# All products of a decoder block with the pass of the low weights last

## The chip, the cores and the metric

The kernel runs on one core of a Trainium2 chip. The metric is the device time of one execution in microseconds, the median of several runs. The core has a matrix engine (TensorE, PE in the profile; its weight loads are PEld), VectorE (DVE), ScalarE (ACT), GpSimd (POOL), and SyncE (SP), which here issues all large transfers. The engines run their own instruction streams in order and meet at semaphores.

## The reference

One decoder block over 1024 tokens with a model width of 1024, in float32. A combined projection gives q, k, v, the conv inputs and the gates. A gated short convolution and a sliding-window attention are merged by sigmoid gates and share the output projection. A SwiGLU FFN of width 2816 follows. Both sub-layers end with a scaled residual and a layer norm.

```python
proj = jnp.einsum('bsd,de->bse', x, w_in[l])
q, k, v, cb, cc, ch, g_conv, g_attn = jnp.split(proj, SPLIT_POINTS, axis=-1)
y_conv = short_conv_mixer(cb, cc, ch, conv_w[l])
y_attn = sliding_window_attention(q, k, v, attn_sinks[l])
merged = jax.nn.sigmoid(g_conv) * y_conv + jax.nn.sigmoid(g_attn) * y_attn
mix = jnp.einsum('bse,ed->bsd', merged, w_out[l])
x = layer_norm(ALPHA * x + mix, ln1_g[l], ln1_b[l])
hid = jax.nn.silu(jnp.einsum('bsd,df->bsf', x, w_gate[l])) * jnp.einsum('bsd,df->bsf', x, w_up[l])
ffn = jnp.einsum('bsf,fd->bsd', hid, w_down[l])
x = layer_norm(ALPHA * x + ffn, ln2_g[l], ln2_b[l])
```

## The kernel before

Every large product is made in three passes over float32r operands. A matrix w is held as w_hi, its rounded value, and w_lo = w - w_hi; the activations likewise as a_hi and a_lo. A product adds w_hi·a_hi, w_hi·a_lo and w_lo·a_hi in one PSUM bank of 128 x 512. `product` (line 1435) does this for one tile of 128 output channels and one half (512) of the tokens: for each of 8 depth tiles (2 for the down projection) three matmuls, lines 1441, 1442, 1443. A product of the projections is thus 24 matmuls. `project` calls it for the input projection, `project_out` for the output projection, `gate_up` and `down` for the FFN. `pair_product` has its own loop of 4 depth tiles with the lines 1662, 1663, 1664; it is one of seven such products by which a pair of halves of gate and up is built, in a loop that takes four of them a pass. `low_last` (line 1425), used for half 0 of the output projection alone, already has another order: lines 1428 and 1429 over all depth tiles, then a wait, then line 1432 eight times.

The high part of a weight tile is copied by ScalarE (semaphores w_hi_s, fw_hi_s, wd_hi_s, ph_s, lines 661, 791, 763, 847, 882) and the low part subtracted by GpSimd after it (w_lo_s, fw_lo_s, wd_lo_s, pl_s, lines 511, 555, 531, 586, 602). `product` is entered after a wait for the low part, which includes the high one. The raw tile is loaded anew when its low part is done.

The order of the work is written out by hand for each engine. Some products have a hook that is called before each depth tile t. In the first product it places transposes of x (`turn_x`), and it waits for parts of the activations: x_lo_s in the first product, m_lo_s in all of half 1 of the output projection (v = 8 to 15), n_lo_s in the first gate/up product of each half. The same hook puts the small matmuls of the first layer norm into the stream (`weave`): the mean over channels (line 1562) before tile 2 of product v=9, the sum of squares (line 1570) before tile 7 of v=11, the spread of the inverse deviation (line 1578) before tile 4 of v=12; and for half 1 of the tokens the same at tile 5 of the first gate/up product and at tiles 3 and 6 of the third:

```python
for v in range(DT, 2 * DT):
    project_out(1, v, v, out_bank(v), {DT + 1: {2: lambda: mean(0)}, DT + 3: {7: lambda: variance(0)},
                                  DT + 4: {4: lambda: spread(0)}}.get(v, {}))
head_hooks = {0: {5: lambda: mean(1)}, 2: {3: lambda: variance(1), 6: lambda: spread(1)}}
```

What these wait for is made elsewhere. VectorE makes the low part of the merged activations, m_lo (line 985), adds a finished output product to the residual (`out_sum`, line 1188), centres (line 1152), adds odd squares (line 1147), scales (line 1176) and makes the low part act_lo (line 1164). ScalarE squares and copies high parts (line 785). GpSimd sums channels (`channel_sum`, line 544) and adds even squares (line 551). Around the first down products VectorE also makes sums and differences of activations for the pair products (line 1259, whose low parts are GpSimd's line 632) and adds the down products to the residual (`add_down`, line 1267); a down product v waits, from v = 4, for sum v-4 to have freed its bank.

Of the kernel before, what the change touches and what calls it, by code (L numbers as in the profile page):

```python
# [106 lines left out]
def build(nc, x, w_in, conv_w, sinks, w_out, ln1_g, ln1_b, w_gate, w_up, w_down, ln2_g, ln2_b, out):  # L107
    ctx = ExitStack()
    with ctx:  # L109
# [185 lines left out]
        def unit_bank(u):  # L295
            return u % 3
# [1126 lines left out]
        def _(pe):  # L1423
# [11 lines left out]
            def product(bank, w_h, w_l, a_hi, a_lo, tiles, ready=None):  # L1435

                for t in range(tiles):
                    if ready is not None:
                        ready(t)
                    hi, lo = folded(a_hi(t)), folded(a_lo(t))  # L1440
                    pe.matmul(bank, w_h(t), hi, start=(t == 0), stop=False)  # L1441
                    pe.matmul(bank, w_h(t), lo, start=False, stop=False)  # L1442
                    last = pe.matmul(bank, w_l(t), hi, start=False, stop=(t == tiles - 1))  # L1443
                return last

            def project(slot, h, bank, ready=None):
                return product(ps[:, bank, :], lambda t: w_hi[:, slot, t], lambda t: w_lo[:, slot, t],
                               lambda t: act_hi[:, t, half(h)], lambda t: act_lo[:, t, half(h)], DT, ready)
# [45 lines left out]
            for n, (t, h) in enumerate(PRO_UNITS):  # L1494
                pe.wait_ge(w_lo_s, t + 1)
# [10 lines left out]
                project(t % 2, h, unit_bank(n + 1), hook).then_inc(unit_s, 1)  # L1506
# [4 lines left out]
            with pe.Fori(0, NKV) as k:  # L1511
                for step, n in STEPS:
                    if step == "unit":
                        if n % 2 == 0:
                            pe.wait_ge(w_lo_s, k * NT + (PRO_TILES + n // 2 + 1))
# [6 lines left out]
                        project((n // 2) % 2, n % 2, unit_bank(n)).then_inc(unit_s, 1)  # L1522
# [59 lines left out]
            def project_out(h, v, w, bank, at={}):  # L1582

                pe.wait_ge(res_s, v + 1)
                if h == 0:
# [5 lines left out]
                pe.wait_ge(w_lo_s, v + (IN_TILES + 1))  # L1591
                return product(ps[:, bank, :], lambda t: out_hi(w)[:, t], lambda t: out_lo(w)[:, t],
                               lambda t: m_hi[h][:, t], lambda t: m_lo[h][:, t], DT,
                               weave(at, lambda t: pe.wait_ge(m_lo_s, DT * h + t + 1))).then_inc(out_s, 1)
# [8 lines left out]
            def gate_up(h, s, ready=None):  # L1603

                if h == 0:
                    pe.wait_ge(fw_lo_s, s + 1)
# [3 lines left out]
                        ready).then_inc(f_s, 1)  # L1610

            def down(i, c, h, m):

                v = h * DT + m
                if m == 0:
                    pe.wait_ge(wd_lo_s, i * 4 + (2 * c + 2))
# [4 lines left out]
                if v >= 4:  # L1621
                    pe.wait_ge(add_s, i * 32 + (16 * c + v - 3))
                product(ps[:, 4 + v % 4, :], lambda t: wd_hi[:, t, blk(m)], lambda t: wd_lo[:, t, blk(m)],
                        lambda t: hid_hi[:, t, half(h)], lambda t: hid_lo[:, t, half(h)], 2).then_inc(d_s, 1)
# [15 lines left out]
            def pair_product(i, c, j):  # L1640
# [4 lines left out]
                pe.wait_ge(pl_s, i * 28 + (n + 1))  # L1645
# [13 lines left out]
                for t in range(4):  # L1659
                    hi, lo = ring(w_hi, n)[:, t], ring(w_lo, n)[:, t]  # L1660
                    b_hi, b_lo = (folded(ap) for ap in right(j, t))
# [70 lines left out]
```

## Time and profile before

| | |
|---|---|
| median of 3 runs | 1383.12 us (1382.83 to 1383.79) |
| the profiled execution, its own time | 1382.94 us |
| its span, first to last instruction | 1381.1 us |
| TensorE busy | 1367.6 us, 6658 matmuls |
| VectorE / GpSimd / ScalarE busy | 780.9 / 596.4 / 484.2 us |
| mean granted TensorE clock | 0.999 |
| moved by DMA | 80.22 MB |

The times of the profile are microseconds from the start of the span; a line number is that of the kernel's text. "idle before" is the time in which the engine did nothing just before an instruction, with what released it. Matmuls are pipelined, and the end of one overlaps the next, so their pace is read from start to start.

### The profile page before, as it was taken

What the parts mean: (1) busy time and instruction counts of PE and PEld (TensorE: products, weight loads), DVE (VectorE), ACT (ScalarE), POOL (GpSimd) and SP (SyncE); (2) the same over time, 40 slices, a digit from 0 to 9 for tenths busy, and PEclk for the clock granted to TensorE, in tenths of its full rate; (3) what the DMA queues carried; (4) which work ended last, traced back from release to release, by engine and by line L of the source; (5) the groups of instructions that cost most, each with busy time, mean ns of one, the idle gap of its engine ahead of it and who ended that gap; (6) DMA issues with size and microseconds to landing.
All of it is one profiled execution on the core that took longest, in us unless ns stands there. A gap on an engine that the chain in (4) does not pass through costs nothing. (4 is left out here: it accounts for less than half of the span.)

```text
span 1381.1 us, 19035 instructions
## 1 busy us (share of the span) xinstructions
PE 1367.6 (99%) x6658; PEld 1201.5 (87%) x6658; DVE 780.9 (57%) x1196; ACT 484.2 (35%) x932; POOL 596.4 (43%) x375
## 2 busy tenths in 40 slices
PE   9999999999999999999999999999999999999997
PEld 8888888888888888888888888888888888888886
DVE  3137564566447653767967935645456454464547
ACT  4434333343243433345245332322323213233143
POOL 2222223212322132124884483754737547475474
PEclk9999999999999999999999999999999999999999
DMA  6111111111111111111430121112211122121113
GB/s 184 57 51 47 34 43 47 44 46 46 46 46 33 43 46 46 46 46 51 132 93 31 46 80 43 61 47 67 68 31 61 53 61 68 32 66 56 52 54 122
DMA packets 128406, 80.22 MB, mean 58 GB/s; under 512 B 8432, under 2 KB 123120, under 8 KB 128368
## 3 DMA queue, kind: packets, MB, share of 16 engines
q1 hardware_dynamic: 128368, 79.73, 19.0%
q8 instruction: 22, 0.36, 0.1%
q14 instruction: 16, 0.13, 0.0%
HBM read 75.53 MB, written 4.19 MB: 58 GB/s over the span
## 5 line engine op out<-in xcount | busy, mean ns | idle before, releaser
L511 POOL TENSOR_TENSOR w_lo<-raw,w_hi 128x1024 fp32r<-128x1024 f32 x54 | 128.3, 2377 | 481.4 <-ACT w_hi L661 481.4
L1441 PE MATMUL ps<-act_hi,w_hi 128*128 128x512 f32 x864 | 329.5, 381 | 1.1 <-DVE act_lo L971 1.1
L1442 PE MATMUL ps<-act_lo,w_hi 128*128 128x512 f32 x864 | 327.7, 379 | 0.0
L1443 PE MATMUL ps<-act_hi,w_lo 128*128 128x512 f32 x864 | 327.7, 379 | 0.0
L602 POOL TENSOR_TENSOR w_lo<-raw,w_hi 128x512 fp32r<-128x512 f32 x80 | 110.3, 1378 | 204.7 <-ACT w_hi L882 204.7
L1443 PEld LDWEIGHTS ps<-act_hi,w_lo 128*128 128x128 f32 x864 | 163.4, 189 | 23.1
L1441 PEld LDWEIGHTS ps<-act_hi,w_hi 128*128 128x128 f32 x864 | 163.4, 189 | 23.0 <-issue 1.3
L1442 PEld LDWEIGHTS ps<-act_lo,w_hi 128*128 128x128 f32 x864 | 163.6, 189 | 21.6
L1441 PE MATMUL ps<-hid_hi,wd_hi 128*128 128x512 f32 x320 | 121.6, 380 | 1.3 <-DVE res L1267 1.3
L1442 PE MATMUL ps<-hid_lo,wd_hi 128*128 128x512 f32 x320 | 121.4, 379 | 0.0
L1663 PE MATMUL ps<-act_lo,w_hi 128*128 128x512 f32 x320 | 121.4, 379 | 0.0
L1664 PE MATMUL ps<-act_hi,w_lo 128*128 128x512 f32 x320 | 121.4, 379 | 0.0
L1443 PE MATMUL ps<-hid_hi,wd_lo 128*128 128x512 f32 x320 | 121.4, 379 | 0.0
L1662 PE MATMUL ps<-act_hi,w_hi 128*128 128x512 f32 x320 | 121.3, 379 | 0.0
L1273 DVE TENSOR_TENSOR res<-res,ps 128x512 f32<-128x512 f32 x128 | 87.3, 687 | 59.9 <-PE ps L1443 59.9
L1663 PE MATMUL ps<-a_lo,w_hi 128*128 128x512 f32 x240 | 91.0, 379 | 0.0
L1664 PE MATMUL ps<-a_hi,w_lo 128*128 128x512 f32 x240 | 91.0, 379 | 0.0
L1662 PE MATMUL ps<-a_hi,w_hi 128*128 128x512 f32 x240 | 91.0, 379 | 0.0
L602 POOL TENSOR_TENSOR w_lo<-w_sum,w_hi 128x512 fp32r<-128x512 f32 x60 | 80.7, 1353 | 9.2 <-ACT w_hi L882 9.2
L661 ACT ACTIVATE w_hi<-raw 128x1024 fp32r<-128x1024 f32 x54 | 57.0, 1055 | 62.6 <-PE ps L1443 62.1
L1118 DVE TENSOR_TENSOR pt_lo<-ps,pt_hi 128x512 fp32r<-128x512 f32 x60 | 38.9, 687 | 64.0 <-ACT pt_hi L741 63.0
L882 ACT ACTIVATE w_hi<-raw 128x512 fp32r<-128x512 f32 x80 | 49.8, 623 | 71.2 <-POOL raw L614 50.6
(205 smaller groups left out, 2514.7 us busy)
## 6 DMA issues: line engine op xcount, KB each, us to landing
raw<-in_w_in SPq DMA_DIRECT2D x52, 512.0 KB, 3.6
raw<-in_w_gate SPq DMA_DIRECT2D x40, 256.0 KB, 2.8
raw<-in_w_up SPq DMA_DIRECT2D x40, 256.0 KB, 3.1
raw_d<-in_w_down SPq DMA_DIRECT2D x20, 512.0 KB, 3.3
raw<-in_w_out SPq DMA_DIRECT2D x16, 512.0 KB, 3.5
xs<-in_x SPq DMA_DIRECT2D x8, 512.0 KB, 8.3
out<-rows SPq DMA_DIRECT2D x7, 512.0 KB, 2.6
raw_first<-in_w_down SPq DMA_DIRECT2D x2, 512.0 KB, 3.7
```

Source lines behind the costliest of these rows:

```text
L511: pool.tensor_tensor(w_lo[:, slot], raw[:, slot], fp(w_hi[:, slot]), ALU.subtract).then_inc(w_lo_s, 1)
L602: pool.tensor_tensor(wide(ring(w_lo, n)), src, fp(wide(ring(w_hi, n))), ALU.subtract).then_inc(pl_s, 1)
L661: act.activation(w_hi[:, slot], raw[:, slot], ACT.Copy).then_inc(w_hi_s, 1)
L882: act.activation(wide(ring(w_hi, n)), src, ACT.Copy).then_inc(ph_s, 1)
L1118: dve.tensor_tensor(pt_lo[:, kb], ps[:, TURN + kb, :], fp(pt_hi[:, kb]), ALU.subtract).then_inc(pt_lo_s, 1)
L1273: dve.tensor_tensor(tile, tile, bank, ALU.add).then_inc(add_s, 1)
L1441: pe.matmul(bank, w_h(t), hi, start=(t == 0), stop=False)
L1442: pe.matmul(bank, w_h(t), lo, start=False, stop=False)
L1443: last = pe.matmul(bank, w_l(t), hi, start=False, stop=(t == tiles - 1))
L1662: pe.matmul(out, hi, b_hi, start=(t == 0 and not on), stop=False, skip_group_check=True)
L1663: pe.matmul(out, hi, b_lo, start=False, stop=False, skip_group_check=True)
L1664: last = pe.matmul(out, lo, b_hi, start=False, stop=(t == 3), skip_group_check=True)
```

## The change

In `product` one loop over the depth tiles becomes two: the first runs both passes of w_hi for each tile, with the hook; then comes a wait, given as the new argument `low`; the second runs the pass of w_lo. `pair_product` is written in the same way. The wait before a product is now for the high part of the weight, and the wait for the low part stands between the loops. Two products of one weight share it, so only the first has the waits, except in the first eight products and in the output projection. `low_last` and the last down products, made as rows, stay as they are.

```diff
@@ -1432,20 +1432,22 @@
                     last = pe.matmul(bank, w_l(t), folded(a_hi(t)), start=False, stop=(t == tiles - 1))
                 return last
 
-            def product(bank, w_h, w_l, a_hi, a_lo, tiles, ready=None):
+            def product(bank, w_h, w_l, a_hi, a_lo, tiles, ready=None, low=None):
 
                 for t in range(tiles):
                     if ready is not None:
                         ready(t)
-                    hi, lo = folded(a_hi(t)), folded(a_lo(t))
-                    pe.matmul(bank, w_h(t), hi, start=(t == 0), stop=False)
-                    pe.matmul(bank, w_h(t), lo, start=False, stop=False)
-                    last = pe.matmul(bank, w_l(t), hi, start=False, stop=(t == tiles - 1))
+                    pe.matmul(bank, w_h(t), folded(a_hi(t)), start=(t == 0), stop=False)
+                    pe.matmul(bank, w_h(t), folded(a_lo(t)), start=False, stop=False)
+                if low is not None:
+                    low()
+                for t in range(tiles):
+                    last = pe.matmul(bank, w_l(t), folded(a_hi(t)), start=False, stop=(t == tiles - 1))
                 return last
 
-            def project(slot, h, bank, ready=None):
+            def project(slot, h, bank, ready=None, low=None):
                 return product(ps[:, bank, :], lambda t: w_hi[:, slot, t], lambda t: w_lo[:, slot, t],
-                               lambda t: act_hi[:, t, half(h)], lambda t: act_lo[:, t, half(h)], DT, ready)
+                               lambda t: act_hi[:, t, half(h)], lambda t: act_lo[:, t, half(h)], DT, ready, low)
 
 
             pe.wait_ge(tables, 2)
@@ -1492,7 +1494,7 @@
                      {0: lambda: turn_x(11), 2: lambda: turn_x(12), 3: lambda: turn_x(13),
                       5: lambda: turn_x(14), 6: lambda: turn_x(15)}]
             for n, (t, h) in enumerate(PRO_UNITS):
-                pe.wait_ge(w_lo_s, t + 1)
+                pe.wait_ge(w_hi_s, t + 1)
                 if n >= 3:
                     if n - 3 < 4:
                         pe.wait_ge(v_copied, n - 2)
@@ -1503,7 +1505,7 @@
                              (lambda c: pe.wait_ge(x_lo_s, 7 + c // 4)) if n == 0 else None)
                 if n > 0:
                     pe.wait_ge(x_lo_s, 16 if h else 8)
-                project(t % 2, h, unit_bank(n + 1), hook).then_inc(unit_s, 1)
+                project(t % 2, h, unit_bank(n + 1), hook, lambda: pe.wait_ge(w_lo_s, t + 1)).then_inc(unit_s, 1)
                 if 1 <= n < 5:
                     turn_v(n - 1)
 
@@ -1511,15 +1513,17 @@
             with pe.Fori(0, NKV) as k:
                 for step, n in STEPS:
                     if step == "unit":
+                        tile, low = k * NT + (PRO_TILES + n // 2 + 1), None
                         if n % 2 == 0:
-                            pe.wait_ge(w_lo_s, k * NT + (PRO_TILES + n // 2 + 1))
+                            pe.wait_ge(w_hi_s, tile)
+                            low = lambda: pe.wait_ge(w_lo_s, tile)
                         if n in (1, 2):
                             pe.wait_ge(k_copied, 8 + 4 * n)
                         if n == 2:
                             pe.wait_ge(prep_dve, k * 9 + 1)
                         if n >= 3:
                             pe.wait_ge(*consumed(k, n - 3))
-                        project((n // 2) % 2, n % 2, unit_bank(n)).then_inc(unit_s, 1)
+                        project((n // 2) % 2, n % 2, unit_bank(n), None, low).then_inc(unit_s, 1)
                     elif step == "scores":
                         if n == 0:
                             pe.wait_ge(prep_dve, k * 9 + 2)
@@ -1588,10 +1592,11 @@
                                     lambda t: m_hi[h][:, t], lambda t: m_lo[h][:, t], DT,
                                     lambda t: pe.wait_ge(m_lo_s, t + 1),
                                     lambda: pe.wait_ge(w_lo_s, v + (IN_TILES + 1))).then_inc(out_s, 1)
-                pe.wait_ge(w_lo_s, v + (IN_TILES + 1))
+                pe.wait_ge(w_hi_s, v + (IN_TILES + 1))
                 return product(ps[:, bank, :], lambda t: out_hi(w)[:, t], lambda t: out_lo(w)[:, t],
                                lambda t: m_hi[h][:, t], lambda t: m_lo[h][:, t], DT,
-                               weave(at, lambda t: pe.wait_ge(m_lo_s, DT * h + t + 1))).then_inc(out_s, 1)
+                               weave(at, lambda t: pe.wait_ge(m_lo_s, DT * h + t + 1)),
+                               lambda: pe.wait_ge(w_lo_s, v + (IN_TILES + 1))).then_inc(out_s, 1)
 
             with pe.Fori(0, DT // OB) as i:
                 for e in range(OB):
@@ -1602,18 +1607,22 @@
 
             def gate_up(h, s, ready=None):
 
+                low = None
                 if h == 0:
-                    pe.wait_ge(fw_lo_s, s + 1)
+                    pe.wait_ge(fw_hi_s, s + 1)
+                    low = lambda: pe.wait_ge(fw_lo_s, s + 1)
                 w_h, w_l = ffn_hi(s), ffn_lo(s)
                 product(ps[:, s, :], lambda t: w_h[:, t], lambda t: w_l[:, t],
                         lambda t: act_hi[:, t, half(h)], lambda t: act_lo[:, t, half(h)], DT,
-                        ready).then_inc(f_s, 1)
+                        ready, low).then_inc(f_s, 1)
 
             def down(i, c, h, m):
 
                 v = h * DT + m
+                low = None
                 if m == 0:
-                    pe.wait_ge(wd_lo_s, i * 4 + (2 * c + 2))
+                    pe.wait_ge(wd_hi_s, i * 4 + (2 * c + 2))
+                    low = lambda: pe.wait_ge(wd_lo_s, i * 4 + (2 * c + 2))
                     if c:
                         pe.wait_ge(pair_s, i * 48 + (STEPS_OF * (2 * c) + (LOW0, LOW1)[h]))
                     else:
@@ -1621,7 +1630,7 @@
                 if v >= 4:
                     pe.wait_ge(add_s, i * 32 + (16 * c + v - 3))
                 product(ps[:, 4 + v % 4, :], lambda t: wd_hi[:, t, blk(m)], lambda t: wd_lo[:, t, blk(m)],
-                        lambda t: hid_hi[:, t, half(h)], lambda t: hid_lo[:, t, half(h)], 2).then_inc(d_s, 1)
+                        lambda t: hid_hi[:, t, half(h)], lambda t: hid_lo[:, t, half(h)], 2, None, low).then_inc(d_s, 1)
 
 
             head_hooks = {0: {5: lambda: mean(1)}, 2: {3: lambda: variance(1), 6: lambda: spread(1)}}
@@ -1642,7 +1651,7 @@
                 n = 7 * c + j
                 before = i * 48 + STEPS_OF * c
                 now = i * 48 + STEPS_OF * (c + 1)
-                pe.wait_ge(pl_s, i * 28 + (n + 1))
+                pe.wait_ge(ph_s, i * 28 + (n + 1))
                 if j == FIRST_HIGH:
                     pe.wait_ge(pair_s, before + GATE0)
                 elif j == SECOND_SUM:
@@ -1657,11 +1666,14 @@
                         FOURTH_DIFF: BY}[j]
                 out, on = ps[:, bank, :], j in (THIRD_DIFF, FIRST_LOW)
                 for t in range(4):
-                    hi, lo = ring(w_hi, n)[:, t], ring(w_lo, n)[:, t]
                     b_hi, b_lo = (folded(ap) for ap in right(j, t))
+                    hi = ring(w_hi, n)[:, t]
                     pe.matmul(out, hi, b_hi, start=(t == 0 and not on), stop=False, skip_group_check=True)
                     pe.matmul(out, hi, b_lo, start=False, stop=False, skip_group_check=True)
-                    last = pe.matmul(out, lo, b_hi, start=False, stop=(t == 3), skip_group_check=True)
+                pe.wait_ge(pl_s, i * 28 + (n + 1))
+                for t in range(4):
+                    last = pe.matmul(out, ring(w_lo, n)[:, t], folded(right(j, t)[0]), start=False, stop=(t == 3),
+                                     skip_group_check=True)
                 last.then_inc(prod_s, 1)
 
             pe.wait_ge(alo_s, 8)
```

How this moves TensorE's instructions is shown at two places. The first is the end of product v=8 of the output projection and the start of v=9 (128x512 is the moving tile; m_hi, m_lo are the merged activations). Before:

```order
L1441 MATMUL ps<-m_hi,w_hi 128x512 [waits m_lo_done]
L1442 MATMUL ps<-m_lo,w_hi 128x512
L1443 MATMUL ps<-m_hi,w_lo 128x512
L1441 MATMUL ps<-m_hi,w_hi 128x512 [waits m_lo_done]
L1442 MATMUL ps<-m_lo,w_hi 128x512
L1443 MATMUL ps<-m_hi,w_lo 128x512
L1441 MATMUL ps<-m_hi,w_hi 128x512 [waits m_lo_done,w_lo_done,res_tile_done]
```

With the change:

```order
L1440 MATMUL ps<-m_hi,w_hi 128x512 [waits m_lo_done]
L1441 MATMUL ps<-m_lo,w_hi 128x512
L1440 MATMUL ps<-m_hi,w_hi 128x512 [waits m_lo_done]
L1441 MATMUL ps<-m_lo,w_hi 128x512
L1445 MATMUL ps<-m_hi,w_lo 128x512 [waits w_lo_done]
L1445 MATMUL ps<-m_hi,w_lo 128x512 x7
L1440 MATMUL ps<-m_hi,w_hi 128x512 [waits m_lo_done,w_hi_done,res_tile_done]
```

The last wait for m_lo stood before the last three matmuls of the product and now stands before its last ten.

The second place is product v=11 with the matmuls of the squares (L1570 before, L1574 in the changed text), up to the start of v=12. Before:

```order
L1441 MATMUL ps<-m_hi,wd_hi 128x512 [waits m_lo_done]
L1442 MATMUL ps<-m_lo,wd_hi 128x512
L1443 MATMUL ps<-m_hi,wd_lo 128x512
L1441 MATMUL ps<-m_hi,wd_hi 128x512 [waits m_lo_done]
L1442 MATMUL ps<-m_lo,wd_hi 128x512
L1443 MATMUL ps<-m_hi,wd_lo 128x512
L1570 MATMUL ps<-mean_of,sq_acc 128x1 [waits odd_squares_step,even_squares_step,m_lo_done]
L1570 MATMUL ps<-mean_of,sq_acc 128x1 x7
L1441 MATMUL ps<-m_hi,wd_hi 128x512
L1442 MATMUL ps<-m_lo,wd_hi 128x512
L1443 MATMUL ps<-m_hi,wd_lo 128x512
L1441 MATMUL ps<-m_hi,w_hi 128x512 [waits m_lo_done,w_lo_done,res_tile_done]
```

With the change:

```order
L1440 MATMUL ps<-m_hi,wd_hi 128x512 [waits m_lo_done]
L1441 MATMUL ps<-m_lo,wd_hi 128x512
L1440 MATMUL ps<-m_hi,wd_hi 128x512 [waits m_lo_done]
L1441 MATMUL ps<-m_lo,wd_hi 128x512
L1574 MATMUL ps<-mean_of,sq_acc 128x1 [waits odd_squares_step,even_squares_step,m_lo_done]
L1574 MATMUL ps<-mean_of,sq_acc 128x1 x7
L1440 MATMUL ps<-m_hi,wd_hi 128x512
L1441 MATMUL ps<-m_lo,wd_hi 128x512
L1445 MATMUL ps<-m_hi,wd_lo 128x512 [waits w_lo_done]
L1445 MATMUL ps<-m_hi,wd_lo 128x512 x7
L1440 MATMUL ps<-m_hi,w_hi 128x512 [waits m_lo_done,w_hi_done,res_tile_done]
```

The squares' matmuls stood after 21 of the 24 matmuls of their product and now stand after 14, with two of the high and eight of the low passes behind them.

## Rows read from the trace of the kernel before

**Rows 1.** The page: busy time, and groups by line (columns as its heads say).
```profile
PE 1367.6 (99%) x6658; PEld 1201.5 (87%) x6658; DVE 780.9 (57%) x1196; ACT 484.2 (35%) x932; POOL 596.4 (43%) x375
...
L1441 PE MATMUL ps<-act_hi,w_hi 128*128 128x512 f32 x864 | 329.5, 381 | 1.1 <-DVE act_lo L971 1.1
...
L1443 PE MATMUL ps<-act_hi,w_lo 128*128 128x512 f32 x864 | 327.7, 379 | 0.0
```

**Rows 2.** TensorE's timeline, output projection half 0: start us, us, engine, line, count.
```profile
648.52 1.89 PE L1432 MATMUL ps<-m_hi,w_lo 128*128 128x512 f32 x8
650.25 0.38 PE L1428 MATMUL ps<-m_hi,w_hi 128*128 128x512 f32 x1
```

**Rows 3.** TensorE's timeline, output projection half 1, products v=8 to v=12.
```profile
681.33 0.38 PE L1441 MATMUL ps<-m_hi,w_hi 128*128 128x512 f32 x1
...
686.51 0.38 PE L1441 MATMUL ps<-m_hi,w_hi 128*128 128x512 f32 x1
...
697.73 0.38 PE L1441 MATMUL ps<-m_hi,wd_hi 128*128 128x512 f32 x1
...
702.26 1.84 PE L1570 MATMUL ps<-mean_of,sq_acc 128*128 128x1 f32 x16
...
704.69 0.38 PE L1441 MATMUL ps<-m_hi,w_hi 128*128 128x512 f32 x1
```

**Rows 4.** VectorE's timeline in the same stretch.
```profile
683.45 2.20 DVE L985 SCALAR_TENSOR_TENSOR m_lo<-res,m_hi 128x512 fp32r<-128x512 f32 x1
...
700.65 1.32 DVE L1147 TENSOR_TENSOR sq_acc<-sq_acc,sq 128x512 f32<-128x512 f32 x1 [0.76 <-ACT sq L776]
```

**Rows 5.** Timelines of VectorE, GpSimd and TensorE up to the mean of half 1.
```profile
710.97 0.69 DVE L1188 SCALAR_TENSOR_TENSOR res<-res,ps 128x512 f32<-128x512 f32 x1 [5.30 <-PE ps L1443]
...
727.57 0.68 DVE L1188 SCALAR_TENSOR_TENSOR res<-res,ps 128x512 f32<-128x512 f32 x1
...
728.33 1.27 POOL L544 TENSOR_TENSOR acc<-acc,res 128x512 f32<-128x512 f32 x1 [1.89 <-DVE res L1188]
...
726.30 0.38 PE L1441 MATMUL ps<-act_hi,w_hi_b 128*128 128x512 f32 x1
...
729.74 1.10 PE L1562 MATMUL ps<-acc,mean_of 128*128 128x512 f32 x2
```

**Rows 6.** Timelines of VectorE and GpSimd, one meeting in that stretch.
```profile
716.67 2.22 DVE L1164 SCALAR_TENSOR_TENSOR act_lo<-res,lnb,act_hi 128x512 fp32r<-128x512 f32 x1
...
715.50 2.84 POOL L555 TENSOR_TENSOR wd_lo<-raw,wd_hi 128x1024 fp32r<-128x1024 f32 x1
```

**Rows 7.** Timelines of VectorE and TensorE, squares and norm of half 1.
```profile
737.96 1.59 DVE L1147 TENSOR_TENSOR sq_acc<-sq_acc,sq 128x512 f32<-128x512 f32 x1
...
756.33 0.75 DVE L1164 SCALAR_TENSOR_TENSOR act_lo<-res,lnb,act_hi 128x512 fp32r<-128x512 f32 x1
...
739.74 0.31 PE L1570 MATMUL ps<-mean_of,sq_acc 128*128 128x1 f32 x2
...
757.13 0.48 PE L1441 MATMUL ps<-act_hi,w_hi_b 128*128 128x512 f32 x1
...
757.88 0.38 PE L1441 MATMUL ps<-act_hi,w_hi_b 128*128 128x512 f32 x1
```

**Rows 8.** Timelines of TensorE and VectorE, first down products.
```profile
773.42 0.38 PE L1441 MATMUL ps<-hid_hi,wd_hi 128*128 128x512 f32 x1
...
786.62 0.48 PE L1441 MATMUL ps<-hid_hi,wd_hi 128*128 128x512 f32 x1 [1.29 <-DVE res L1267]
...
774.92 0.69 DVE L1267 SCALAR_TENSOR_TENSOR res<-res,ps 128x512 f32<-128x512 f32 x1
...
784.23 1.74 DVE L1259 SCALAR_TENSOR_TENSOR w_sum<-res,b_diff 128x512 f32<-128x512 f32 x1 [0.58 <-POOL a_lo L632]
785.89 0.67 DVE L1267 SCALAR_TENSOR_TENSOR res<-res,ps 128x512 f32<-128x512 f32 x1
```

## The prediction

> **What bounds the kernel now.** I read the busy shares first [rows 1]: TensorE is busy 1367.6 of 1381.1 us. No other engine is near that, so a change can gain or lose only where TensorE waits, or comes to wait. Next I read the groups of instructions by line. Before the 864 matmuls on L1441 there is 1.1 us of idle time in all, at the very start, for act_lo. Before the low pass on L1443 there is none: nothing in the profile waits for the low part of a weight. Then I read the timeline of TensorE from start to start, because the printed 379 ns of one matmul overlap the next. Matmuls of 512 columns start 0.216 us apart. Last I read the timeline from 680 to 790 us, where half 1 of the output projection, the norm between the sub-layers, the first gate/up products and the first down products meet. There VectorE and GpSimd make operands just in time, and TensorE has most of its few stalls.
>
> **What the new order costs by itself.** Nothing is added but one semaphore wait in a product; the matmuls and weight loads keep their number. The trace of before has such products already: half 0 of the output projection runs L1428/L1429 over the depth, waits, and runs L1432 eight times [rows 2]. These eight take 1.73 us from their first start to the next product's, 0.216 each, so a product of 24 takes 24 x 0.216 = 5.18 us; in the old order it takes 681.33 to 686.51, 5.18 us too [rows 3]. Bounds: zero by these rows; and if each mid-product wait made the pipeline restart as a stall does (three matmuls then take 0.75, not 0.65 us [rows 7]), 0.1 us for each of some 220 waits, 23 us. Rows 2 show this very operation, so I take zero.
>
> **What the moved waits gain.** The wait for a low part comes up to 16 matmuls later. It was never the last to end, so this gains nothing in the steady loops. At the first product the wait that ends last is for act_lo, and it stays.
>
> **What they lose.** Products with a wait at each depth tile, or with a small matmul hooked in (mean, squares, spread of the inverse), now reach tile t after 2t matmuls, not 3t. They ask for a late operand up to 7 x 0.216 = 1.51 us sooner, and when they then stall, eight low matmuls still lie behind. I follow D, the delay of TensorE, through the places in order.
>
> (a) Product v=8, the first of half 1, starts at 681.33 [rows 3]. Its last tile needs m_lo of tile 7, which VectorE finishes at 683.45 + 2.20 = 685.65 [rows 4]. Before, tile 7 was reached at 681.33 + 21 x 0.216 = 685.87, just behind that. Now it is reached at 684.35, waits to 685.70, and then come 0.32 + 0.216 + 8 x 0.216 = 2.26 us (0.32 is the first distance after a stall: 0.75 - 2 x 0.216 [rows 7]). Product 9 starts at 687.96 instead of 686.51: D = 1.45.
>
> (b) VectorE's centring follows product 9, so the chain of the squares is late by 1.45 too and ends at 700.65 + 1.32 + 1.45 = 703.42 [rows 4]. Product 11 starts at 697.73 + 1.45 = 699.18 and reaches the squares' matmul L1570, hooked before tile 7, after 14 matmuls at 702.20; before, 21 matmuls covered the chain (702.26 against 701.97). It waits to 703.48. From L1570 to the next product it was 704.69 - 702.26 = 2.43 with three matmuls in it [rows 3]; now there are ten, so 2.43 + 7 x 0.216 = 3.94. Product 12 starts at 707.43: D = 2.74.
>
> (c) The mean L1562 of half 1, hooked at tile 5 of the first gate/up product, waits for a sum on GpSimd that follows VectorE's last out_sum. VectorE's chain to there starts when product 12 ends (710.97 [rows 5]), so it starts 2.74 late; call X what is left of that when GpSimd's sum ends at 728.33 + 1.27 [rows 5]. In between VectorE is disturbed: its L1164 at 716.67 takes 2.22 us [rows 6], the undisturbed one at 756.33 takes 0.75 [rows 7]. The disturbed one ends 0.55 after GpSimd's L555 does (715.50 + 2.84 = 718.34). I read that as a lock: of two such operations the later one runs its last 0.55 us behind the other. GpSimd's queue is late by only 1.45 here, so they meet otherwise than before. Laid out in turn, the first four L1164 end at 717.08, 719.84, 721.54 and 722.21, late by 2.7, 3.7, 2.7 and 1.6 (the fourth meets nothing, since GpSimd waits for a high part), and the last out_sum starts at 729.40 instead of 727.57: X = 1.83. Bounds: 0.5, if the meetings nearly vanish, and 2.74, if each stays. The mean starts at 729.74 + 1.83 = 731.57. TensorE is there at 726.30 + 2.74 + 10 x 0.216 = 731.20 and waits 0.37. Behind the mean lay 9 matmuls and now lie 14: D = 1.83 + 5 x 0.216 = 2.91.
>
> The Trainium skill (SBUF — State Buffer, section "SBUF: two separate sides") states that a VectorE operation with two SBUF inputs and a GpSimd operation exclude each other for a whole instruction. By that rule the sum is the forecast; were the printed durations carried along as they stand, the end would be some 0.9 us later. Rows 6 speak for the rule.
>
> (d) The squares of half 1 stand at tile 3 of their product (739.74), and their chain ends at 737.96 + 1.59 + 1.83 = 741.38 [rows 7]. TensorE arrives at 739.74 - 3 x 0.216 + 2.91 = 742.00: no stall, 0.6 us to spare, and L1570 is 2.26 late. The spread follows after six matmuls instead of nine, so it is 2.26 - 0.65 = 1.61 late, and so is VectorE's norm of half 1 behind it.
>
> (e) The first product of half 1 meets this norm tile by tile. The last act_lo is now done at 756.33 + 0.75 + 1.61 = 758.69 [rows 7]. Tile 7 starts at 758.74 and the next product 2.26 later, at 761.0; before these were 757.13 and 757.88. D = 3.12.
>
> (f) The down products start at 773.42 + 3.12 [rows 8]. Before, the tenth stalls until 786.62 for VectorE's sum L1267, with 1.45 over the spacing. A late TensorE could be absorbed there. But VectorE's first sum (774.92) waits for the first down product (773.42 + 6 x 0.216 = 774.72), so VectorE becomes 3.12 late as well. Its own later wait for GpSimd, at 784.23, is 0.58 us. Without the lock this would bring the sum at 785.89 to 3.12 - 0.58 = 2.54 late; laid out with it, VectorE meets GpSimd's next operation again and the sum is 3.07 late. I take 3.07; bounds 3.12 - 1.45 = 1.67, and 3.12.
>
> (g) In the pair loop, from there to the rows at the end, TensorE waits for nothing and so gives nothing back.
>
> **Sum.** +1.45 (a) +1.29 (b) +0.17 (c) +0.21 (e) -0.05 (f) = +3.07 us. The profiled execution ran 1382.94 us, its span of 1381.1 and 1.8 around it; that gives 1386.0. It lies 0.18 below the median of 1383.12, from which the same sum gives 1386.2. I forecast 1386.1, 0.22% over the median. A measurement of this kernel can tell about 0.2%, 2.8 us, from no change.
>
> **Rivals.**
> - VectorE catches up. If X is 0.5, nobody waits for the mean, D stays about 2.5 after (c) and 2.8 after (e), and the stall at the tenth down product absorbs up to 1.45: +1.3, 1384.4 us. For it: VectorE's own wait of 0.58 and long disturbed operations that may shrink. Against it: VectorE's first sum is bound to TensorE in (f). It is the case of not slower, and it decides once (c) and (f) give back 0.3 us more than I count. Chance 0.30, for all from +1.0 to +2.5.
> - All disturbed durations stay, X = 2.74: D = 3.8 after (c) and 4.0 at the end, 1387.0 us. Chance 0.12.
> - Nothing stalls, because the operands of (a) and (b) come sooner than the rows say: 1383.1 us. The rows leave 0.2 to 0.3 us to spare where 1.5 is taken. Chance 0.03.
> - Some wait for a low part was binding after all: at most the 1.1 us of the start, 1382.0 us. Chance 0.01.
> - Every mid-product wait restarts the pipeline: +23 us, 1406 us. All of rows 2 is against it. Chance 0.01.
> - The forecast, +2.5 to +3.6: 0.53, of which four fifths lie over 2.8.
>
> Slower by over 0.2% has 0.43 + 0.12 + 0.01 and a little of the first rival's edge, 0.58; within 0.2% has 0.40, faster 0.02. The range goes from the first rival to just above the second, 1384.3 to 1387.2.
>
> **What would show it.** In the changed kernel's profile: eight low matmuls in 1.73 us and products of 5.18 us in the steady loops; about 1.3 us idle before the last tile of product v=8, released by VectorE's m_lo; about 1.3 more before L1570 of half 0, and a short one before the mean of half 1; no idle time before any low pass; the first down product 3.1 us later than 773.42, and the same time from the first pair product to the end. Wrong would be: idle time before a low pass, a pair loop of another length, or a stall at the tenth down product that is shorter than before by what the others grew.

## The result and the profile after

| | before | after |
|---|---|---|
| median, 7 runs each | 1383.29 us (1382.66 to 1383.79) | 1387.74 us (1387.61 to 1389.13) |
| the profiled execution, its span | 1382.94, 1381.1 us | 1389.13, 1387.3 us |
| mean granted clock of the profiled execution | 0.999 | 0.996 |

The ratio of the mean times is 1.0035, 95% interval [1.0024, 1.0046]: slower. The medians lie 4.45 us apart where +3.07 was forecast, and 1387.74 is 1.6 us above the forecast time (1386.1; range to 1387.2). Of the seven executions of after, five took 1387.6 to 1387.8 us and two 1389.0 to 1389.1; the profiled one is of the two.

The page first, answering to [rows 1]:

```profile
PE 1370.8 (99%) x6658; PEld 1202.9 (87%) x6658; DVE 778.7 (56%) x1196; ACT 484.2 (35%) x932; POOL 593.6 (43%) x375
...
L1440 PE MATMUL ps<-act_hi,w_hi 128*128 128x512 f32 x864 | 329.3, 381 | 1.1 <-DVE act_lo L971 1.1
...
L1445 PE MATMUL ps<-act_hi,w_lo 128*128 128x512 f32 x864 | 204.1, 379 | 0.0
```

The low pass waits for nothing. But TensorE is *busy* 3.2 us longer for the same 6658 matmuls, and this must make the reader suspicious: a stall lengthens the span, not the busy time. (The 204.1 on L1445 is no gain: eight overlapping records in a row are joined.)

TensorE's timeline at product v=8, answering to [rows 3]:

```profile
681.07 0.38 PE L1440 MATMUL ps<-m_hi,w_hi 128*128 128x512 f32 x1
...
685.44 0.48 PE L1440 MATMUL ps<-m_hi,w_hi 128*128 128x512 f32 x1 [1.18 <-DVE m_lo L985]
...
685.98 1.89 PE L1445 MATMUL ps<-m_hi,w_lo 128*128 128x512 f32 x8
687.70 0.38 PE L1440 MATMUL ps<-m_hi,w_hi 128*128 128x512 f32 x1
```

The stall before the last tile is there, and the product takes 6.63 us instead of 5.18: +1.45. The same view at product v=11 and the start of v=12:

```profile
701.73 0.38 PE L1441 MATMUL ps<-m_lo,wd_hi 128*128 128x512 f32 x1
703.32 2.51 PE L1574 MATMUL ps<-mean_of,sq_acc 128*128 128x1 f32 x16 [1.21 <-DVE sq_acc L1147]
705.69 0.77 PE L1440 MATMUL ps<-m_hi,wd_hi 128*128 128x512 f32 x1
706.26 0.63 PE L1441 MATMUL ps<-m_lo,wd_hi 128*128 128x512 f32 x1
706.68 3.62 PE L1445 MATMUL ps<-m_hi,wd_lo 128*128 128x512 f32 x8
710.10 0.63 PE L1440 MATMUL ps<-m_hi,w_hi 128*128 128x512 f32 x1
...
711.34 0.38 PE L1441 MATMUL ps<-m_lo,w_hi 128*128 128x512 f32 x1
```

The squares start at 703.32. The forecast was 703.48; this whole execution is 0.26 early at the start of v=8 (681.07 against 681.33), so they start 0.10 later than forecast. Then something is there that no step of the prediction has: the eight low matmuls take 3.42 us from start to next start, 0.427 each, where at v=8 they take 1.72. The next view is TensorE's busy time and granted clock by stretches: us, then busy time of PE, PEld, DVE, ACT and POOL, then PEclk, the DMA share and GB/s.

```profile
701.00:703.00 2.00, 1.11 (x6) 0.62 (x4) 1.25 (x2) 1.98 (x4) 1.65 (x2) 1.00 0.00 0
703.00:705.00 2.00, 1.68 (x13) 1.71 (x14) 0.77 (x2) 1.07 (x1) 2.00 (x1) 0.86 0.00 0
705.00:707.00 2.00, 2.00 (x7) 1.82 (x8) 0.00 (x0) 1.14 (x2) 2.00 (x2) 0.50 0.13 39
707.00:709.00 2.00, 2.00 (x6) 1.55 (x6) 0.00 (x0) 0.07 (x1) 2.00 (x2) 0.50 0.83 243
...
711.00:713.00 2.00, 2.00 (x13) 1.82 (x12) 0.12 (x2) 1.06 (x1) 1.86 (x3) 0.93 0.00 0
```

The granted clock falls while the one-column matmuls of the squares run, stays at 0.50 (1.2 of 2.4 GHz), and is back by 711.34. In this stretch 11 distances of 0.427 instead of 0.216 cost 2.32 us, two in between 0.44, and the squares themselves run 0.59 slower (2.37 against 1.78 us to the next matmul in the kernel with a filler, below): 3.35 us in all.

Of the rest of the road, timelines of TensorE, GpSimd and VectorE at the mean of half 1, and of TensorE at the first gate/up product of half 1 and at the tenth down product, answering to [rows 5, 7, 8]:

```profile
734.69 1.10 PE L1566 MATMUL ps<-acc,mean_of 128*128 128x512 f32 x2
...
733.27 1.27 POOL L544 TENSOR_TENSOR acc<-acc,res 128x512 f32<-128x512 f32 x1 [3.70 <-DVE res L1188]
...
732.50 0.69 DVE L1188 SCALAR_TENSOR_TENSOR res<-res,ps 128x512 f32<-128x512 f32 x1 [0.19 <-PE ps L1445]
...
759.63 0.48 PE L1440 MATMUL ps<-act_hi,w_hi_b 128*128 128x512 f32 x1 [0.45 <-DVE act_lo L1164]
...
760.95 0.48 PE L1440 MATMUL ps<-act_hi,w_hi_b 128*128 128x512 f32 x1 [0.62 <-DVE act_lo L1164]
...
761.83 0.48 PE L1440 MATMUL ps<-act_hi,w_hi_b 128*128 128x512 f32 x1 [0.18 <-DVE act_lo L1164]
...
792.77 0.48 PE L1440 MATMUL ps<-hid_hi,wd_hi 128*128 128x512 f32 x1 [1.30 <-DVE res L1267]
```

TensorE is now so late that VectorE's last out_sum waits 0.19 for it. At the tenth down product the stall is as long as before (1.30 against 1.29): nothing is absorbed.

How late each product starts against before, in us, taken from the traces and counted from the start of v=8 (the start of v=8 itself lies up to 0.3 us off that of before in these three):

| start of | forecast | after | after, again | filler ahead |
|---|---|---|---|---|
| v=9 | 1.45 | 1.45 | 1.45 | 1.45 |
| v=12 | 2.74 | 5.66 | 4.20 | 2.91 |
| v=13 | 2.74 | 6.25 | 4.57 | 2.91 |
| second gate/up product | 2.91 | 6.28 | 4.59 | 2.94 |
| second gate/up product of half 1 | 3.12 | 6.46 | 4.79 | 3.13 |
| tenth down product to the end | 3.07 | 6.40 | 4.73 | 3.06 |

### The profile page after: what moved, and what is told of

It reads as the page before. It is cut to its first block and busy times, and to the rows that moved or that the text cites. A ratio compares the mean times of both kernels' runs of the same rounds, so it can differ in the third digit from the quotient of the medians.

```text
span 1387.3 us, 19035 instructions
## 1 busy us (share of the span) xinstructions
PE 1370.8 (99%) x6658; PEld 1202.9 (87%) x6658; DVE 778.7 (56%) x1196; ACT 484.2 (35%) x932; POOL 593.6 (43%) x375
## 3 DMA queue, kind: packets, MB, share of 16 engines
HBM read 75.53 MB, written 4.19 MB: 57 GB/s over the span
## 5 line engine op out<-in xcount | busy, mean ns | idle before, releaser
L1445 PE MATMUL ps<-act_hi,w_lo 128*128 128x512 f32 x864 | 204.1, 379 | 0.0
L1445 PEld LDWEIGHTS ps<-act_hi,w_lo 128*128 128x128 f32 x864 | 163.3, 189 | 23.2
L1445 PE MATMUL ps<-hid_hi,wd_lo 128*128 128x512 f32 x320 | 95.2, 379 | 0.0
L1675 PE MATMUL ps<-act_hi,w_lo 128*128 128x512 f32 x320 | 82.1, 379 | 0.0
L1440 PEld LDWEIGHTS ps<-hid_hi,wd_hi 128*128 128x128 f32 x320 | 60.5, 189 | 10.8 <-DVE res L1267 2.0
```

Source lines behind the costliest of these rows:

```text
L1440: pe.matmul(bank, w_h(t), folded(a_hi(t)), start=(t == 0), stop=False)
L1445: last = pe.matmul(bank, w_l(t), folded(a_hi(t)), start=False, stop=(t == tiles - 1))
L1675: last = pe.matmul(out, ring(w_lo, n)[:, t], folded(right(j, t)[0]), start=False, stop=(t == 3), skip_group_check=True)
```

## Experiments

Each was timed in alternation with the kernel before on the same chip; the medians of before were 1382.90 to 1383.07. The ratios are those of the mean times. "Delay" is counted as in the table above.

**The old order where operands are awaited.** The steady loops keep the new order; only v=8 to 15 and the gate/up products get the old loop and the old place of the wait.

```diff
+def product_mixed(bank, w_h, w_l, a_hi, a_lo, tiles, ready=None, low=None):
+    if low is not None: low()
+    for t in range(tiles):
+        if ready is not None: ready(t)
+        ... (w_hi·a_hi, w_hi·a_lo, w_lo·a_hi of tile t)
-    return product(...)            # in project_out, h == 1, and in gate_up
+    return product_mixed(...)
```

> The new order everywhere except where a product has operands that come tile by tile or a hooked-in matmul: half 1 of the output projection (v=8 to 15) and all gate/up products are in the old order again, with the wait for the low part ahead. About 200 products keep the new order. Theory (the order and the mid-product wait cost nothing, all loss is in the timed products): the time of before, 1383.3 us, within 0.3. Rival (each mid-product wait or the repeated high weights cost a little, 10 ns a product): 1385.3 us, and growing distances in the head loop and the pair loop.

Measured: 1383.17 us, ratio 1.0001 [0.9992, 1.0010]; delay 0.0 at every mark. The new order costs nothing in the input projection, the down and the pair products, and gains nothing. The whole loss lies in these 16 products.

**Old order for v=11 alone.** This takes away the stall at the squares and leaves every other effect: `project_out` calls `product_mixed` where v == DT + 3.

> The changed kernel with product v=11 alone in the old order, so that the squares' matmuls stand after 21 matmuls again. Theory (TensorE's clock falls because an idle gap of 1.3 us and the 16 one-column matmuls behind it come together): no gap before the squares, no stretch at the low clock; product 9 and product 12 are both 1.45 us late, the mean and the norm of half 1 add up to 1: the end is 1.5 to 2.7 us later than before, 1384.8 to 1386.0. Rival (the clock falls because of the new order itself): still a low stretch after the squares, about 1387.

**Six more 512-column matmuls in the squares' hook, ahead of the wait.** They write a bank that nobody reads and cover the idle time.

```diff
 def variance(q):
+    if q == 0:
+        for _ in range(6):
+            pe.matmul(ps[:, 4, :], out_hi(DT + 3)[:, 0], folded(m_hi[1][:, 0]), start=True, stop=True)
     pe.wait_ge(even_s, 3 * (q + 1))
     pe.wait_ge(odd_s, 3 * (q + 1))
```

> The changed kernel with six extra matmuls of 512 columns (1.30 us, into a spare bank, never read) just ahead of the wait for the squares in product v=11, where TensorE else idles 1.2 us. They change nothing in the operands' times. Theory: the idle gap is filled, the clock stays at 2.4 GHz, product 12 is about 2.8 us late against 5.66, and the end is at my forecast without the clock, 1386.2 to 1386.6. Rival (the clock falls for another reason than the gap): 1387.7 to 1389 as the changed kernel.

**The same six behind the wait**, between the idle time and the one-column matmuls.

> The changed kernel with the same six extra matmuls behind the wait for the squares, ahead of the one-column matmuls: the idle gap stays, but the one-column matmuls no longer follow it directly. Theory (gap and one-column matmuls must be adjacent): clock stays at 2.4 GHz, product 12 is 2.8 + 1.3 = 4.1 us late, the end +4.0 to +4.5, 1387.3 to 1387.8. Rival A (the gap alone lowers the clock): the six run at half pace, product 12 about 7 us late, 1390 or more. Rival B (the one-column matmuls alone lower it): they are at half pace and what follows too, also about 1390.

Measured: v=11 in the old order 1385.59 us, ratio 1.0020 [1.0010, 1.0029]; filler ahead 1386.33, 1.0025 [1.0015, 1.0034]; filler behind 1387.48, 1.0032 [1.0020, 1.0044]. The windows view for 704 to 712 us, one fence for each kernel: before, after, v=11 in the old order, filler ahead, filler behind:

```profile
704.00:712.00 8.00, 8.00 (x42) 7.15 (x43) 1.81 (x4) 3.33 (x4) 7.86 (x6) 1.00 0.45 132
```

```profile
704.00:712.00 8.00, 8.00 (x29) 6.78 (x29) 0.78 (x2) 3.15 (x5) 7.86 (x5) 0.57 0.45 132
```

```profile
704.00:712.00 8.00, 8.00 (x48) 7.30 (x48) 0.78 (x2) 3.07 (x5) 7.86 (x5) 1.00 0.44 132
```

```profile
704.00:712.00 8.00, 8.00 (x47) 7.28 (x47) 0.78 (x2) 2.86 (x4) 7.86 (x5) 1.00 0.45 132
```

```profile
704.00:712.00 8.00, 8.00 (x49) 7.36 (x50) 1.16 (x3) 2.98 (x5) 7.86 (x4) 1.00 0.44 132
```

The third number from the end is the clock: 0.57 in after, 1.00 in the others. TensorE's timeline with the filler behind the wait:

```profile
703.94 1.53 PE L1574 MATMUL ps<-m_hi,wd_hi 128*128 128x512 f32 x6 [1.21 <-DVE sq_acc L1147]
705.31 1.84 PE L1577 MATMUL ps<-mean_of,sq_acc 128*128 128x1 f32 x16
...
707.52 1.89 PE L1445 MATMUL ps<-m_hi,wd_lo 128*128 128x512 f32 x8
709.25 0.38 PE L1440 MATMUL ps<-m_hi,w_hi 128*128 128x512 f32 x1
```

The idle time is the 1.21 us of after, the one-column matmuls are the same sixteen records, and the low pass runs at 0.216 a matmul. The single executions say the same: in the kernels with v=11 old, with either filler and with the moved hook (below), all 37 have a mean granted clock of 0.998 or 0.999, as before, and the spans of one kernel differ by 1.3 us at most, less than a fall costs; in after, 13 of the 14 on record have 0.996 or 0.997. So neither the idle time nor the one-column matmuls lower the clock alone; it falls where one follows the other directly. Both fillers put six wide matmuls close by, so what is shown is that these are enough to keep the clock; how near the idle time and the one-column matmuls must be to each other is not shown. The filler behind the wait costs its own 6 x 0.216 = 1.30 us (delay at v=12: 4.19 against 2.91), which is why its median is close to that of after. The filler ahead is after without the fall, and the table shows the forecast's sum in it: 3.06 us at the end.

**Parts of the new order alone.** First only the gate/up products new; then only v=8; then only v=11, the others old.

> The changed kernel with half 1 of the output projection (v=8 to 15) in the old order and the gate/up products in the new one: only the places (c) to (f) of the forecast are left, and TensorE is in time until the mean of half 1. Theory: the mean starts when before, and five more matmuls lie behind it (+1.08); the norm of half 1 comes 0.22 sooner, and the first product of half 1 ends 2.26 after its last act_lo: +1.29; all of it stays at the down products, whose stall hides none: +1.1 to +1.3 at the end, 1384.1 to 1384.3. Rival (the stall of the tenth down product absorbs it): +0.0 to +0.3, 1383.0 to 1383.3.

> Of the timed products v=8 alone has the new order; v=9 to 15 and all gate/up products have the old one. Theory: product 9 is 1.45 us late, the squares' chain too, so nothing stalls further in the output projection; the clock stays at 2.4 GHz; at the mean of half 1 some 0.2 is given back: +1.2 to +1.5 at the end, 1384.2 to 1384.5. Rival (a gap of 1.2 us is enough for the clock to fall, or VectorE's chain does not follow and the delay is absorbed): +3 or more, or about 0.

> Of the timed products v=11 alone, the one with the squares' matmuls, has the new order. Theory (gap of 1.2 us and one-column matmuls behind it lower the clock): product 9 in time, then the gap before the squares, a stretch at the low clock of up to 6 us, product 12 late by 1.3 + 1.4 to 2.9 = 2.7 to 4.2 us, and the end the same, 1385.6 to 1387.2. Rival (the fall of the clock needs the earlier gap of product v=8 as well): product 12 late by 1.3 to 1.5, the end 1384.3 to 1384.6.

Measured: gate/up alone 1384.34 us (1.0009 [0.9999, 1.0019]), delay 1.04 behind the mean and 1.17 at the end; v=8 alone 1384.58 (1.0012 [1.0003, 1.0022]), delay 1.45 at v=9 and 1.43 at the end. The two add up to 2.6, and the kernel with only v=11 old, which has just these two, ends 2.64 late. v=11 alone has a median of 1384.70 (1.0019 [1.0009, 1.0029]): this misses the 1385.6 to 1387.2 that I expected and lies just above the rival's 1384.3 to 1384.6, by which the fall needs the stall of v=8 as well. But six of its ten executions lie at 1384.2 to 1384.9 and four at 1386.0, 1386.9, 1387.9 and 1389.8. The profiled one took 1386.86:

```profile
702.15 1.92 PE L1587 MATMUL ps<-mean_of,sq_acc 128*128 128x1 f32 x16 [1.21 <-DVE sq_acc L1147]
...
704.58 3.44 PE L1445 MATMUL ps<-m_hi,wd_lo 128*128 128x512 f32 x8
707.85 0.38 PE L1456 MATMUL ps<-m_hi,w_hi 128*128 128x512 f32 x1
```

Here too the clock falls (low pass 3.27 us) and costs 1.69 us, with the same 1.21 us idle. Only this execution has a trace, but span and mean granted clock are on record for each. The six faster ones have spans of 1381.9 to 1382.5 us at 0.998 or 0.999. The four others have 1383.9 and 1384.0 us (0.998 and 0.997) and 1386.1 and 1386.3 us (0.996 both). The three steps fit no fall, the short one and the long one; the rest of the 1389.8 lies outside the span. The fall is thus not certain to come: four times in ten here. With the stall of v=8 ahead of it, it came in both traced executions of after, and of its fourteen timed ones only one, at 1385.87 us and a clock of 0.999, lies where the sum without a fall would put it. So the stall of v=8 is not needed for a fall; whether it makes one likelier, and what else decides it, stays open.

**The changed kernel again.**

> The changed kernel once more, for the clock: five of its seven executions took 1387.7 us and two 1389.1, with mean clocks of 0.997 and 0.996. Theory: the gap before the squares is the same in all of them, but the stretch at the low clock is longer or shorter, so an execution of 1387.7 has product 12 late by about 4.2 instead of 5.7 us and all other distances unchanged. Rival: the two kinds differ somewhere else than after the squares.

Measured: 1387.77 us (1385.87 to 1389.26), 1.0034 [1.0022, 1.0045]. Its profiled execution took 1387.88:

```profile
703.00:705.00 2.00, 1.24 (x12) 1.27 (x12) 1.21 (x2) 1.50 (x2) 2.00 (x2) 1.00 0.00 0
705.00:707.00 2.00, 2.00 (x13) 1.75 (x13) 0.00 (x0) 1.21 (x2) 2.00 (x2) 0.86 0.05 10
707.00:709.00 2.00, 2.00 (x6) 1.64 (x5) 0.00 (x0) 0.00 (x0) 2.00 (x2) 0.50 0.86 251
709.00:711.00 2.00, 2.00 (x9) 1.65 (x9) 0.78 (x2) 0.93 (x1) 2.00 (x2) 0.79 0.88 261
```

The clock falls 2 us later and for a shorter time: 7 distances of 0.427 and two in between, 1.69 us, against 3.35. That is the difference between its end (4.73 late) and the other's (6.40), and the likely reason for the two groups of times in the first seven runs, whose mean clocks are 0.997 (the five) and 0.996 (the two).

**The new order everywhere, with the hook moved.** The squares go from tile 7 of v=11 to tile 0 of v=12, ten matmuls later, the spread from tile 4 to tile 7 of v=12.

```diff
-    {DT + 1: {2: lambda: mean(0)}, DT + 3: {7: lambda: variance(0)}, DT + 4: {4: lambda: spread(0)}}
+    {DT + 1: {2: lambda: mean(0)}, DT + 4: {0: lambda: variance(0), 7: lambda: spread(0)}}
```

> The changed kernel with all products in the new order; only the hooks of the squares and of the spread of half 0 are moved: the squares' one-column matmuls from ahead of tile 7 of product v=11 to ahead of tile 0 of v=12 (ten matmuls later), the spread from tile 4 to tile 7 of v=12. The chain of the squares ends at about 703.4 us on the clock of before; the squares are now reached at about 704.4. Theory (the clock falls only when an idle gap is followed directly by the one-column matmuls): no gap there, the clock stays at 1.00 between 704 and 712 us, the start of v=12's tile 0 is 1.45 us later than before and not 5.7, and the end 2.7 us later as in the run with v=11 in the old order: 1385.5 us, at most 1386.0. Rival (the new order lowers the clock there whatever stands ahead of the one-column matmuls): clock 0.5 for some us again and 1387 to 1388 us. Rival (the later spread holds up the norm of half 0): a new stall at the first gate/up product and more than 1386.5 us with the clock at 1.00.

```profile
702.34 1.89 PE L1445 MATMUL ps<-m_hi,wd_lo 128*128 128x512 f32 x8
704.07 1.84 PE L1574 MATMUL ps<-mean_of,sq_acc 128*128 128x1 f32 x16
705.77 0.46 PE L1440 MATMUL ps<-m_hi,w_hi 128*128 128x512 f32 x1
```

Measured: 1385.66 us (1385.13 to 1386.18), 1.0019 [1.0009, 1.0028], clock 1.00 from 704 to 712, delay 2.62 at the end. No idle time ahead of the squares, no fall: 2.1 us of the loss come back in a kernel whose products are all in the new order.

**Could the place be made faster than before?** The tenth down product has a stall of 1.29 to 1.31 us in every kernel so far [rows 8]. Three kernels, all built on the one with the old order: VectorE's sums of down products put ahead of its differences; with that, the first two gate/up products of half 1 made together tile by tile; with both, the low wait of the pair products put back ahead of their first matmul.

```diff
-for t in range(4):
-    depth_difference(t)
-    if t < 3:
-        add_down(0, 0, 3 + t, "first")
+for t, sums in enumerate(((3, 4), (5, 6), (7,), (8,))):
+    for v in sums:
+        add_down(0, 0, v, "first")
+    if t < 4:
+        depth_difference(t)
 ...
-for v in range(6, 2 * DT):
+for v in range(9, 2 * DT):
     add_down(0, 0, v, "first")
```

> Timed products in the old order as in e5, and on VectorE another order of work around the first down products: the sums of the down products 3 to 8 come ahead of the differences for the pair products, which are needed 6 us later. Theory (the tenth down product waits only for VectorE's order of work): its stall of 1.45 us and the 0.07 behind it are gone, the pair loop starts 1.5 us sooner, 1381.5 us. Rival (the late differences hold up the first pair products through GpSimd): TensorE waits there instead, 1382.5 to 1383.5.

> As e8, and the first two gate/up products of half 1 are made together, tile by tile (six matmuls, 1.30 us, for each tile of act_lo that VectorE delivers in 1.32 us). Theory: the waits of the first product of half 1 (1.83 us over the spacing) are gone as well, and the pair loop starts 3.3 us sooner than before. Its first product finds its high part ready, and its low part, done about 1.7 us after the start, is just in time because the wait stands behind the high passes: 1379.6 to 1380.2. Rival (VectorE's sums hold up the down products then): 1381 to 1381.5.

> As e9, but each pair product waits for its low part ahead of its first matmul, as before the change; its order of passes stays. Theory: the first pair product now waits for GpSimd's low part, about 1.5 to 2 us, and this stays to the end: 1381.2 to 1382.0. Rival (the low part is there in time anyway, and where the wait stands makes no difference): the time of e9.

Measured: 1382.96, 1383.32 and 1382.92 us, ratios 1.0001 [0.9992, 1.0010], 1.0004 [0.9995, 1.0013] and 1.0000 [0.9991, 1.0009]. All three gains failed to arrive: 1381.5, 1379.6 to 1380.2 and 1381.2 to 1382.0 were expected. They were there: counted from v=8 as above, the tenth down product starts 1.6, 3.4 and 3.4 us earlier than before. They are gone before the second pair of halves is under way. TensorE with the sums first, and ScalarE and VectorE ahead of it:

```profile
816.49 0.48 PE L1685 MATMUL ps<-a_hi,w_hi 128*128 128x512 f32 x1 [1.40 <-DVE u_st L1344]
...
811.53 0.63 ACT L882 ACTIVATE w_hi<-w_sum 128x512 fp32r<-128x512 f32 x1 [3.50 <-POOL w_sum L610]
...
812.72 1.80 DVE L1319 SCALAR_TENSOR_TENSOR hid_lo<-t_g,hid_hi 128x512 fp32r<-128x512 f32 x1 [2.35 <-ACT hid_hi L904]
```

VectorE waits 2.35 us for ScalarE's hid_hi, which stands in ScalarE's queue behind a copy of w_sum that waits 3.50 us for GpSimd. GpSimd is busy 19.18 of the 20 us from 796 to 816 (17.78 before), so it has little left to catch up with. And it starts 1.8 us later than before. GpSimd's first sum for the pair products and VectorE's last difference ahead of it, in the kernel before and then with the sums first:

```profile
789.92 1.28 POOL L607 TENSOR_TENSOR w_sum<-raw 128x512 f32<-128x512 f32 x1 [0.30 <-POOL a_lo L632]
...
786.49 0.74 DVE L1259 SCALAR_TENSOR_TENSOR w_sum<-res,b_diff 128x512 f32<-128x512 f32 x1
```

```profile
791.68 1.28 POOL L607 TENSOR_TENSOR w_sum<-raw 128x512 f32<-128x512 f32 x1 [0.30 <-POOL a_lo L632]
...
787.61 1.75 DVE L1259 SCALAR_TENSOR_TENSOR w_sum<-res,b_diff 128x512 f32<-128x512 f32 x1 [0.59 <-POOL a_lo L632]
```

GpSimd's a_lo must follow that difference, which now ends at 789.36 and ended at 787.23 before. This is the rival that I named for the first of the three kernels, the late differences holding up the pair products through GpSimd, and the median of 1382.96 lies in its 1382.5 to 1383.5.

In the second and third kernel part of the gain is lost already at the fourteenth down product, which waits for a sum that VectorE makes behind its last difference. TensorE in the third kernel, there and at the first pair product:

```profile
789.80 0.48 PE L1441 MATMUL ps<-hid_hi,wd_hi 128*128 128x512 f32 x1 [1.51 <-DVE res L1267]
...
795.27 0.48 PE L1695 MATMUL ps<-act_hi,w_hi 128*128 128x512 f32 x1 [1.32 <-POOL w_lo L602]
```

So some 1.5 us of the 3.4 end in the wait for VectorE's sums, and most of the rest in waits that lead to GpSimd: at 816.80 in the second kernel (1.39 us), at the first pair product in the third. Where the wait for the low part stands only moves the place. Whether the rest could be had with the differences in time, or by relieving GpSimd, is open; no run parts the two.

## Why the prediction was right in part and wrong in its time

- **Bound, and price of the order (zero).** Right: 0.0 with the old order in the awaited products, and no idle time ahead of a low pass.
- **(a) v=8, +1.45.** Right to the digit, and v=8 alone carries 1.43 of it to the end.
- **(b) The squares.** The stall is right (start within 0.10 us of the forecast, 1.21 idle). The step that failed is the sentence behind it: "From L1570 to the next product it was 704.69 - 702.26 = 2.43 with three matmuls in it [rows 3]; now there are ten, so 2.43 + 7 x 0.216 = 3.94." It took 6.78 in the first trace of after and 5.33 in the second. I priced the ten matmuls at the clock of a stretch that had no idle time ahead of the one-column matmuls. With the fall taken away, by the filler ahead of the wait, the stretch takes 4.02, and the kernel is 2.91 late at v=12 (2.74 forecast) and 3.06 at the end (3.07 forecast). The 0.17 too much at v=12 does not reach the end, because the wait for the mean takes it up. No rival had the clock, so the range ended at 1387.2, where the median lies 0.5 above. The fall costs 1.69 or 3.35 us in the traced executions.
- **(c) The lock and X.** In after it is moot, since TensorE is later than VectorE's chain. With the filler ahead the last out_sum starts at 729.12, 1.87 late counted from v=8; laid out with the lock I had 1.83, with the printed durations carried along 2.74. The stall ahead of the mean is what counts: with the squares' stall gone the end is only 0.42 earlier (2.64 against 3.06), because TensorE then waits 1.11 us for the mean.
- **(d), (e), (f), (g).** Right: no idle time ahead of the second squares; +0.19 for (e), forecast 0.21, though in three short waits and not in one; -0.07 for (f), forecast -0.05; a constant delay from there to the end.
- **The rivals.** "VectorE catches up" (0.30) is refuted: nothing was given back at (c), and at most 0.07 at (f), in any kernel with the new gate/up order. "Disturbed durations stay" (0.12) is too: X was 1.87 with the filler ahead, not 2.74.

The Trainium skill (TensorE: Matmul & The Clock Gate, section "A second HAM failure mode: psum-queue depth-cycling") states of another kernel (bf16) that short but frequent idle times between its groups of matmuls send the clock to its lower level and back. Here two idle times of 1.2 us, 18 us apart, are ahead of the fall in after, and only the one with one-column matmuls behind it brings it; with v=11 alone one such idle time was enough. That passage would have made a rival.

## What to carry to other kernels

A wait placed earlier within a product costs the cover of the matmuls that moved behind it, and in a kernel at 99% TensorE each such wait is worth reading out to a tenth of a microsecond; move the hooks along with the order, so that small matmuls meet their operand late rather than early. Where a forecast puts an idle time directly ahead of very narrow matmuls, price the matmuls behind it at both levels of the clock. And a gain at one stall is real only if the engine that feeds the next stage, here GpSimd, has slack there as well and is not made late by the same edit.

## What the runs showed of the hardware that I had not expected

- About 1.2 us of idle TensorE followed directly by one-column matmuls (1.8 us of them) lowered the granted clock from 1.00 to 0.50 in all three traced executions that had it. By spans and mean clocks on record it did so in 13 of 14 executions of after, but in only 4 of 10 with v=11 alone. Idle times of 1.1 to 1.3 us with 512-column matmuls behind them did not (v=8, the mean with v=11 old, the tenth down product, the filler behind the wait), nor the same one-column matmuls without it (before, v=11 in the old order, filler ahead, the moved hook).
- At 0.50 matmuls of 512 columns start 0.427 us apart, at 1.00 0.216. In the traces the clock stayed low for 6.8 us (after) or 3.4 us (after again, v=11 alone); when it fell and for how long differed between executions of one kernel.
- A kernel's times can therefore lie in groups 1.3 us and more apart: 1387.7 and 1389.1 in after, where the two traces show the same waits ahead of the squares, and spans of about 1382.3, 1384.0 and 1386.2 with v=11 alone, where only one execution is traced.
